# A mixture-of-experts stage that gathers raw rows and scales them afterwards, with an eighth down-weight buffer and three dummy matmuls moved

## The chip, the core and the metric

The kernel is one program on 1 NeuronCore of one Trainium2 chip. The metric is the device time of one execution in microseconds (us). Five engines run their own instruction streams and meet at semaphores: TensorE (PE), VectorE (DVE), ScalarE (ACT), GpSimd (POOL) and SyncE (SP). SP issues nearly all plain transfers; POOL issues the indirect ones. All transfers share the core's 16 DMA engines.

## The reference, cut to what matters

The reference is two transformer blocks, one after the other, on one sequence of 512 tokens of width 1024, all in float32. The change touches only the end of the second block, its mixture of experts:

```python
def rms_norm_2(x, g):
    y = x * lax.rsqrt(jnp.mean(x * x, axis=-1, keepdims=True) + EPS)
    return y * g

# in second_block, after the mixer has updated x
h = modulate(rms_norm_2(x, norm2_g[l]), shift2, scale2)      # h * (1 + scale) + shift
x = x + gate2[:, None, :] * hierarchical_moe(h, ...)
return rms_norm_2(x, final_norm_g)

def hierarchical_moe(h, ...):           # T = 512 tokens, 32 experts in 4 groups, top 2
    ...                                 # router: group, then two experts in it, weights
    order = jnp.argsort(flat_e)         # the 1024 (token, expert) pairs, by expert
    ...
    xg = ht[slot_tok].reshape(n_blocks, MOE_BLOCK, D)         # gathered token rows
    def run_block(args):
        xb, e, wb = args
        a = jax.nn.silu(xb @ w_gate[e]) * (xb @ w_up[e])      # 1024 -> 256
        return (a @ w_down[e]) * wb[:, None]                  # 256 -> 1024
    out = lax.map(run_block, (xg, blk_expert, slot_w))
    y = jnp.zeros((T, D)).at[slot_tok].add(out)
```

The root of the norm, `rsqrt(mean(x*x) + EPS)`, is one number per token. It can be multiplied into a row before it is gathered or after.

## The kernel before, in words

**The stage.** For the experts the kernel works in blocks of 64 rows (`BS`). Blocks 0 to 31 belong to experts 0 to 31. An expert with more than 64 rows gets further blocks, which run in a loop of up to 16 turns (`OVER`); in the profiled input two of them are needed. Block b goes like this:

- POOL gathers the 64 rows of block b from DRAM into the tile `raw` (line 860, `raw<-xn_rows,arena`). Four buffers (`AHEAD`) hold gathered rows: the gather for block b + 4 is issued once the rows of block b have been turned.
- PE turns the 64 rows in eight transposes (`rows_turned`, line 2806), DVE multiplies and adds the modulation (`scale_shift`, lines 2098 and 2100).
- PE multiplies with gate and up (`gate_up`, line 2790, 32 records in the profile), ACT makes a tanh of the gate half (line 1304), DVE finishes the product (lines 2105, 2107).
- PE turns that (`act_turned`, line 2813), ACT copies it to SBUF (line 1296), PE multiplies with down (`down`, line 2798). DVE applies the residual gate (line 2114) and POOL scatters the rows to `y_rows` (line 865).

PE runs ahead by one block: gate and up of block b, then the turned product, the rows of block b + 2 and the down product of block b - 1.

**The weights.** Gate and up of one expert are one transfer of 2 MB (`expert_gu`, line 626), down is one of 1 MB (`expert_dn`, line 630). There are 7 buffers for each (`NSLOT`). SP's program sets their order. In its steady loop it waits until gate and up of block b are multiplied, issues gate and up of expert b + 7, waits until down of block b is multiplied, and issues down of expert b + 7. Ahead of that loop it issues the first seven of each by hand, in between other work: the transfers of down 2 and 3, gate/up 4, the copy of the residual tile `X` to DRAM (`x_spill`, line 702), a copy of the normed rows to DRAM (`xn_rows`, line 704), down 4 and 5, gate/up 5, then a wait for the first two gathers, down 6, and gate/up 6.

**The routing.** Between the last dense matmul and the first expert block lies the routing: a chain of small DVE instructions with a few small matmuls, which ends in `slot_i` (the token of each slot) and, later, `bexp_i` (the experts of the loop's blocks). The normed rows that the gathers read are made by ACT (line 1285, four instructions) and stored by SP. In the chain's gaps PE runs matmuls that nothing reads (`hold`, line 2754): 10, then 7, then 5 ahead of the first turned rows, and 3 behind the first two blocks' rows.

**The end.** After the last block, `x_spill` comes back to `X`, the two expert rows of each token are read from `y_rows`, weighted and added, and the final norm is written out.

Of the kernel before, what the change touches and what calls it, by code (L numbers as in the profile page):

```python
# [26 lines left out]
P = 128  # L27
# [46 lines left out]
NSLOT = 7  # L74
WS = 4
# [202 lines left out]
def build(nc, x, wp, par_d, con_d, smw_d, bias_d, par2_d, smw2_d, tab2_d, tab3_d, wexp, out):  # L278
    with ExitStack() as ctx:
# [38 lines left out]
        x_spill = nc.dram_tensor("x_spill", (P, NT * D), F32).ap()  # L318
# [161 lines left out]
        def AT(n):  # L480
            at[0] += n
            assert at[0] <= 18560
            return AR(at[0] - n, n)

# [10 lines left out]
        w1c, w2c = AT(NT), AT(NT)  # L495
# [11 lines left out]
        bexp_i = AT(OVER).bitcast(I32)  # L507
        slot_i = AT(NBLK + AHEAD).bitcast(I32)
        pair_i = AT(NBLK + AHEAD).bitcast(I32)
# [4 lines left out]
        idxc, idxp = AT(WS).bitcast(I32), AT(WS).bitcast(I32)  # L514
        nblkf = AT(1)
        nblk_i = AT(1).bitcast(I32)
        actf = AT(2 * P).rearrange("p (u n) -> p u n", u=2)
# [9 lines left out]
        ssf, msf, rsf = AT(NT), AT(NT), AT(NT)  # L527
        ssf2 = AT(NT)
# [80 lines left out]

        def over_slot(v):  # L610

            s = (NE - WS + v) % NSLOT
            return s, 16 * len(range(s, NE, NSLOT))

# [8 lines left out]
        def _(sp):  # L623
# [4 lines left out]
            def expert_dn(b):  # L628

                sp.dma_start(wdn[b % NSLOT], wexp[b, :, 2 * PIECE:WE]).then_inc(S(f"down_loaded{b % NSLOT}"), 16)  # L630
# [10 lines left out]
            for n, p in enumerate(ORDER):  # L641
# [39 lines left out]
                if p == ("wout", 0):  # L681
                    sp.wait_ge(S("values_summed"), A0 + len(aunits))
                    sp.dma_start(X[:, :], x_spill).then_inc(S("x_back"), 16)
# [18 lines left out]
            sp.dma_start(x_spill, X[:, :]).then_inc(S("x_spilled"), 16)  # L702
            sp.wait_ge(S("rows_normed"), NT)
            sp.dma_start(xn_rows.rearrange("(t p) n -> p t n", p=P), xn).then_inc(S("xn_stored"), 16)
# [4 lines left out]
            for v in range(2):  # L709
                sp.wait_ge(S(f"xg_loaded{v}"), 16)  # L710
            expert_dn(6)
            sp.wait_ge(S("x_spilled"), 32)
            expert_gu(6)
            for b in range(NE - NSLOT):
# [3 lines left out]
                expert_dn(b + NSLOT)  # L718
            sp.wait_ge(S("bexp_ready"), 1)
            blocks = sp.value_load(nblk_i[0:1, :], min_val=0, max_val=OVER)  # L720
            with sp.Fori(0, OVER // WS) as i:
                for v in range(WS):
                    with sp.If(WS * i + v < blocks):
# [5 lines left out]
                        sp.wait_ge(S("y_ready"), NE - WS + WS * i + v + 1)  # L729
                        sp.dma_start(wdn[s].rearrange("p (o n) -> p o n", o=1),  # L730
                                     wexp[bass.ds(e, 1), :, 2 * PIECE:WE].rearrange("o p n -> p o n")).then_inc(S(f"down_loaded{s}"), 16)
            sp.wait_ge(S("up_ready"), 28)
            sp.dma_start(X[:, :], x_spill).then_inc(S("x_back"), 16)
# [18 lines left out]
        def _(pool):  # L752
# [118 lines left out]
            for b in range(NE + 3):  # L871
# [3 lines left out]
                if b >= 3:  # L875
                    pool.wait_ge(S("y_copied"), b - 2)
                    scatter((b - 3) % 2, pair_i[:, b - 3:b - 2])
            pool.wait_ge(S("bexp_ready"), 1)
            blocks = pool.value_load(nblk_i[0:1, :], min_val=0, max_val=OVER)
            with pool.Fori(0, OVER // WS) as i:  # L880
                for v in range(WS):
                    with pool.If(WS * i + v < blocks):
# [4 lines left out]
                        pool.wait_ge(S("idx_ready"), 2 * (WS * i + v) + 2)  # L887
# [16 lines left out]
        def _(act):  # L904
# [372 lines left out]
            for t in range(2):  # L1277
                act.activation(xn[:, t, :], Xv[:, t, :], ACT.Square, accum_out=ss2[:, t:t + 1])
            for n in range(5):
                turned(n)  # L1280
            act.activation(xn[:, 2, :], Xv[:, 2, :], ACT.Square, accum_out=ss2[:, 2:3]).then_inc(S("ss_x"), 1)
# [1747 lines left out]
```

## Time and profile before

| | us |
|---|---|
| median of 3 runs | 1617.65 |
| lowest and highest | 1617.4, 1620.41 |
| the profiled execution | 1618.26 |
| its span in the profile | 1616.4 |

The profile is of one execution. Its span, from the first to the last recorded instruction, is 1.86 us shorter than that execution's own time. Over the whole span PE is busy for 1513.8 us, DVE for 777.5, POOL for 585.6 and ACT for 455.3. The mean granted clock of PE is 0.976 of its full 2.4 GHz. The experts take the last fifth of the span, from about 1320 us.

### The profile page before, as it was taken

Reading aid. Unit: us, or ns where it says so; the run is one execution under the profiler, and the core shown is the slowest. Engines: PE = TensorE matmul, PEld = TensorE weight load, DVE = VectorE, ACT = ScalarE, POOL = GpSimd, SP = SyncE. Lnnn points to the kernel's source line nnn. Section 1 sums busy time; section 2 is a strip of 40 time slices with the busy share of each in tenths; the row PEclk is TensorE's granted clock in tenths of the full one; section 3 lists DMA queues with packets and bytes.
Section 4 is the critical chain, followed back from the end, with each engine's and each line's share of the span. In section 5 each row is a group of like instructions: output and inputs, shape, how many; then the busy total and the mean of one; then the engine's idle time right before and its main releaser. Section 6 shows DMA issues by size and latency. Waiting matters only on the chain.

```text
span 1616.4 us, 21298 instructions
## 1 busy us (share of the span) xinstructions
PE 1513.8 (94%) x8362; PEld 1197.2 (74%) x8362; DVE 777.5 (48%) x1490; ACT 455.3 (28%) x734; POOL 585.6 (36%) x483
## 2 busy tenths in 40 slices
PE   7999998999999999999999999999999989977785
PEld 6978887878888888877888888775688866544452
DVE  5565657278686863244615601445313354432234
ACT  4342335242231323252313332342223210000001
POOL 5551220435454444543633154520244313322122
PEclk9998999999999999999999999999999999999998
DMA  4340110325445442232221122310043799999995
GB/s 175 110 186 27 53 53 1 131 107 205 183 156 209 158 181 104 97 118 78 90 98 67 42 79 104 101 51 15 27 182 130 276 357 361 372 397 369 395 410 204
DMA packets 37348, 260.92 MB, mean 161 GB/s; under 512 B 7280, under 2 KB 7920, under 8 KB 13184
## 3 DMA queue, kind: packets, MB, share of 16 engines
q1 hardware_dynamic: 31488, 251.13, 41.1%
q0 software_dynamic: 5760, 8.41, 1.6%
q8 instruction: 68, 1.11, 0.3%
q14 instruction: 32, 0.26, 0.0%
HBM read 252.69 MB, written 17.30 MB: 167 GB/s over the span
## 4 chain that ended last, share of the span: by engine, by line
PE 84%; DVE 7%; issue 4%; ACT 3%; POOL 1%; DMA 1%; DVEq 0%; SPq 0%; ACTq 0%; POOLq 0%
PE G L2205 13%; PE G L2207 13%; PE G L2206 13%; PE SA L2790 4%; PE G L2790 4%; PE SA L2205 3%; PE SA L2207 3%; PE SA L2206 3%; PE PB L2207 3%; PE PB L2205 3%; PE PB L2206 3%; PE OB L2402 2%; PE G L2253 1%; PE SA L2670 1%; PE PB L2798 1%
## 5 line engine op out<-in xcount | busy, mean ns | idle before, releaser
L769 POOL TENSOR_TENSOR wl<-raw,wh 128x512 fp32r<-128x512 f32 x352 | 477.1, 1388 | 685.1 <-ACT wh L920 675.4
L920 ACT ACTIVATE wh<-raw 128x2048 fp32r<-128x2048 f32 x90 | 172.3, 1915 | 284.4 <-PE SA L2207 145.3
L2205 PE MATMUL G<-Hh,wh 128*128 128x512 f32 x544 | 217.3, 399 | 1.7 <-DVE arena L1613 1.4
L2207 PE MATMUL G<-Hh,wl 128*128 128x512 f32 x544 | 213.6, 393 | 0.0
L2206 PE MATMUL G<-Hl,wh 128*128 128x512 f32 x544 | 213.4, 392 | 0.0
L1684 DVE SCALAR_TENSOR_TENSOR arena<-arena,st 128x256 f32<-128x256 f32 x144 | 133.0, 923 | 5.1
L2205 PEld LDWEIGHTS G<-Hh,wh 128*128 128x128 f32 x544 | 103.2, 190 | 22.4 <-issue 2.2
L2207 PEld LDWEIGHTS G<-Hh,wl 128*128 128x128 f32 x544 | 103.0, 189 | 22.4
L2206 PEld LDWEIGHTS G<-Hl,wh 128*128 128x128 f32 x544 | 103.1, 190 | 19.6
L860 POOL DMA_INDIRECT raw<-xn_rows,arena x38 | 36.6, 963 | 130.9 <-PE G L2806 106.7
L2205 PE MATMUL G<-wh,Hh 128*128 128x256 f32 x256 | 77.3, 302 | 1.2 <-POOL wl L769 1.2
L2207 PE MATMUL G<-wh,Hl 128*128 128x256 f32 x256 | 72.7, 284 | 0.0
L2206 PE MATMUL G<-wl,Hh 128*128 128x256 f32 x256 | 72.6, 284 | 0.0
L2205 PE MATMUL G<-Yh,wh 128*128 128x512 f32 x168 | 65.6, 390 | 1.6 <-DVE Yl L1880 1.6
L865 POOL DMA_INDIRECT y_rows<-arena x34 | 34.5, 1014 | 87.1 <-DVE arena L2114 83.1
L1006 ACT ACTIVATE arena<-arena,st 128x128 f32<-128x128 f32 (+3 forms) x64 | 35.9, 561 | 104.8 <-DVE st L1572 104.8
L2207 PE MATMUL G<-Yh,wl 128*128 128x512 f32 x168 | 65.4, 389 | 0.0
L2206 PE MATMUL G<-Yl,wh 128*128 128x512 f32 x168 | 65.4, 389 | 0.0
L1581 DVE COPY arena<-PB 128x128 f32<-128x128 f32 (+3 forms) x64 | 31.3, 489 | 51.6 <-PE PB L2392 51.3
L2205 PE MATMUL SA<-wh,Yh 128*128 128x512 f32 x134 | 53.6, 400 | 0.0
L2207 PE MATMUL SA<-wh,Yl 128*128 128x512 f32 x134 | 52.4, 391 | 0.0
L2205 PEld LDWEIGHTS G<-wh,Hh 128*128 128x128 f32 x256 | 49.2, 192 | 4.2 <-issue 2.9
(536 smaller groups left out, 3094.6 us busy)
## 6 DMA issues: line engine op xcount, KB each, us to landing
raw<-in_pieces_dram SPq DMA_DIRECT2D x91, 1024.0 KB, 4.8
arena<-in_pieces_dram SPq DMA_DIRECT2D x24, 1024.0 KB, 4.8
arena<-in_wexp_dram SPq DMA_DIRECT2D x11, 2048.0 KB
dn_w<-in_wexp_dram SPq DMA_DIRECT2D x18, 1024.0 KB, 41.4
arena<-in_wexp_dram SPq DMA_DIRECT2D x12, 1024.0 KB
gu_y<-in_wexp_dram SPq DMA_DIRECT2D x6, 2048.0 KB
gu_z<-in_wexp_dram SPq DMA_DIRECT2D x5, 2048.0 KB
gu_h<-in_wexp_dram SPq DMA_DIRECT2D x4, 2048.0 KB, 37.8
```

Source lines behind the costliest of these rows:

```text
L769: ins = pool.tensor_tensor(low_[:, part], whole[:, part], high[:, part], ALU.subtract)
L860: pool.indirect_dma_start(xg(v), None, xn_rows, bass.IndirectOffsetOnAxis(ap=index, axis=0), bounds_check=T - 1, oob_is_err=False).then_in ...
L865: pool.indirect_dma_start(y_rows, bass.IndirectOffsetOnAxis(ap=index, axis=0), yb[:, u, :], None, bounds_check=4 * T - 1, oob_is_err=False ...
L920: act.activation(split_pair(s)[0], wait_raw(act, sp_list[s]), ACT.Copy).then_inc(S("high_split"), 1)
L1006: act.activation(SP[:, u % 2, 0:nk], SP[:, u % 2, 0:nk], ACT.Exp, scale=-1.0, bias=nmax[:, u % 2:u % 2 + 1], accum_out=rsum[:, ((u // 8) % ...
L1581: dve.tensor_copy(PTs[:, u % 2, 0:nk], PB[u % 2][:, 0:nk]).then_inc(S("pt_copied"), 1)
L1684: own(dve.scalar_tensor_tensor(a, w[:, k, :], condc[:, k:k + 1], a, ALU.mult, ALU.add))
L2205: pe.matmul(out, ah, bh, start=first, stop=False)
L2206: pe.matmul(out, ah, bl, start=False, stop=False)
L2207: return pe.matmul(out, al, bh, start=False, stop=last)
L2402: ins = pe.matmul(OB[:, h * HD:(h + 1) * HD], PTs[:, u % 2, k * P:(k + 1) * P], Zv[:, k, ty, (h // 4) * HD:(h // 4 + 1) * HD], start=k == ...
L2790: ins = pe.matmul(GU[u][BS * j:BS * j + BS, 0:256], xgT[:, u, k, :], wg[:, j, k, :], start=k == 0, stop=k == KT - 1)
```

## The change

Four things change.

1. The normed copy of the rows is gone: ACT's four instructions, their DRAM tensor and SP's transfer. The gathers read `x_spill`, the raw rows, which is now laid out by token. The root is multiplied into each gathered block by ACT, in place in `raw` (`rows_scaled`), and PE waits for that (`xg_scaled`) in place of the gather. ACT does it for block b + 2, ahead of the tanh of block b.
2. The root of each slot (`row_rstd`) is found like its token: DVE makes `slot_rstd` in two instructions, PE multiplies it with `place` in 16 small matmuls, DVE copies the result. POOL copies the column for each block of the loop.
3. An eighth buffer for down weights (`NDOWN`) lies in the routing's temporaries; the small tables that live on have moved to the end of the arena (`KEPT`). The first seven are issued in another order: down 6 goes ahead of gate/up 4, gate/up 6 no longer comes behind a wait for two gathers, and down 7 follows once the routing is done. The steady loop then issues gate/up of expert b + 7 and down of expert b + 8.
4. The three dummy matmuls behind the first rows are put ahead of them: `hold(8)` in place of `hold(5)` and `hold(3)`.

```diff
+NDOWN = 8
...
-        xn_rows = nc.dram_tensor("xn_rows", (T, D), F32).ap()
         y_rows = nc.dram_tensor("y_rows", (2 * T * 2, D // 2), F32).ap()
-        xn = raw[:, :].rearrange("p (t n) -> p t n", t=NT)
+        sq_act, sq_vec = raw[:, 0:D], raw[:, D:2 * D].unsqueeze(1).to_broadcast([P, NT, D])
+        slot_one = AR(13824, 8 * (NBLK + 2)).rearrange("p (c n) -> p c n", c=8)
+        slot_rstd = AR(14336, 8 * (NBLK + 2)).rearrange("p (c n) -> p c n", c=8)
...
+        row_rstd = KEPT(NBLK + AHEAD)
+        over_rstd = KEPT(WS)
...
+        wdn.append(AR(low_at[0] - PIECE, PIECE))
+        assert low_at[0] - PIECE >= 14848 + 1024
...
             wait_used(sp, ("wout", 2))
             expert_dn(2)
             expert_dn(3)
+            sp.wait_ge(S("low_split"), len(split_pieces()))
+            expert_dn(6)
             wait_group(sp, "wout", 7)
             expert_gu(4)
             wait_freed(sp, "wout", 7)
-            sp.dma_start(x_spill, X[:, :]).then_inc(S("x_spilled"), 16)
-            sp.wait_ge(S("rows_normed"), NT)
-            sp.dma_start(xn_rows.rearrange("(t p) n -> p t n", p=P), xn).then_inc(S("xn_stored"), 16)
+            sp.dma_start(x_spill_tiles, Xv).then_inc(S("x_spilled"), 16)
             expert_dn(4)
             expert_dn(5)
             wait_group(sp, "gr", 0)
             expert_gu(5)
-            for v in range(2):
-                sp.wait_ge(S(f"xg_loaded{v}"), 16)
-            expert_dn(6)
             sp.wait_ge(S("x_spilled"), 32)
             expert_gu(6)
+            sp.wait_ge(S("bexp_ready"), 1)
+            expert_dn(7)
             for b in range(NE - NSLOT):
                 sp.wait_ge(S("up_ready"), b + 1)
                 expert_gu(b + NSLOT)
                 sp.wait_ge(S("y_ready"), b + 1)
-                expert_dn(b + NSLOT)
-            sp.wait_ge(S("bexp_ready"), 1)
+                if b + NDOWN < NE:
+                    expert_dn(b + NDOWN)
...
-            pool.wait_ge(S("xn_stored"), 16)
+            pool.wait_ge(S("x_spilled"), 32)
...
-                pool.indirect_dma_start(xg(v), None, xn_rows, bass.IndirectOffsetOnAxis(ap=index, axis=0),
+                pool.indirect_dma_start(xg(v), None, x_spill, bass.IndirectOffsetOnAxis(ap=index, axis=0),
...
+                        pool.tensor_copy(over_rstd[:, v:v + 1], row_rstd[:, bass.ds(b + AHEAD, 1)]).then_inc(S("idx_ready"), 1)
...
-            act.wait_ge(S("rstd_x"), 6)
-            for t in range(NT):
-                act.activation(xn[:, t, :], Xv[:, t, :], ACT.Copy, scale=rstd2[:, t:t + 1]).then_inc(S("rows_normed"), 1)
...
+            def rows_scaled(b, v, scale):
+
+                act.activation(xg(v), xg(v), ACT.Copy, scale=scale).then_inc(S("xg_scaled"), 1)
+
+            act.wait_ge(S("places_ready"), 3)
+            for b in range(2):
+                act.wait_ge(S(f"xg_loaded{b}"), 16)
+                rows_scaled(b, b, row_rstd[half_rows(b), b:b + 1])
             for b in range(NE):
+                v = (b + 2) % AHEAD
+                act.wait_ge(S(f"xg_loaded{v}"), xg_count(b + 2))
+                rows_scaled(b + 2, v, row_rstd[half_rows(v), b + 2:b + 3])
                 if b >= 1:
                     turned_copy(b - 1)
                 act.wait_ge(S("up_ready"), b + 1)
...
                         act.wait_ge(S("tanh_free"), b - 1)
                         act.activation(tanhg[:, u, :], GU[u][0:BS, 0:256], ACT.Tanh, scale=0.5).then_inc(S("tanh_ready"), 1)
+                        n = (v + 2) % WS
+                        act.wait_ge(S(f"xg_loaded{n}"), xg_count(NE) + 16 * i + 16 * ((v + 2) // WS))
+                        rows_scaled(b + 2, n, over_rstd[half_rows(n), n:n + 1])
                         act.wait_ge(S("act_turned"), b + 1)
...
+            for k in range(2):
+                ins = dve.tensor_tensor(slot_rstd[:, 4 * k:4 * k + 4, :], slot_one[:, 4 * k:4 * k + 4, :],
+                                        rstd2.unsqueeze(2).to_broadcast([P, NT, NBLK + 2]), ALU.mult)
+            ins.then_inc(S("places_ready"), 1)
...
+            dve.wait_ge(S("slots_rooted"), 1)
+            own(dve.tensor_copy(row_rstd[:, 0:NBLK + 2], SA[1][:, 0:NBLK + 2]))
+            dve.tensor_copy(over_rstd, row_rstd[:, NE:NE + WS]).then_inc(S("places_ready"), 1)
...
+            pe.wait_ge(S("places_ready"), 2)
+            for c in range(8):
+                for u in range(2):
+                    ins = pe.matmul(SA[1][BS * u:BS * u + BS, 0:NBLK + 2], place[:, c, :], slot_rstd[:, c, :], start=c == 0, stop=c == 7)
+            ins.then_inc(S("slots_rooted"), 1)
...
-                pe.wait_ge(S(f"xg_loaded{b % AHEAD}"), xg_count(b))
+                pe.wait_ge(S("xg_scaled"), b + 1)
...
-            hold(5)
+            hold(8)
             rows_of(0)
             rows_of(1)
-            hold(3)
```

How the order moves, on three engines. On SP, the transfers between the last weights of the dense part and the steady loop, before (`gu` tiles and 128x4096 are gate/up weights, 128x2048 are down weights, `X` is the seventh gate/up buffer):

```order
L630 DMA dn_w<-in_wexp_dram 128x2048 x2
L626 DMA gu_h<-in_wexp_dram 128x4096
L702 DMA x_spill<-X 128x4096
L704 DMA xn_rows<-raw 128x4x1024
L630 DMA dn_w<-in_wexp_dram 128x2048 x2
L626 DMA gu_l<-in_wexp_dram 128x4096
L630 DMA raw<-in_wexp_dram 128x2048
L626 DMA X<-in_wexp_dram 128x4096
L626 DMA arena<-in_wexp_dram 128x4096
L630 DMA arena<-in_wexp_dram 128x2048
```

And the same place now:

```order
L652 DMA dn_w<-in_wexp_dram 128x2048 x2
L652 DMA raw<-in_wexp_dram 128x2048
L648 DMA gu_h<-in_wexp_dram 128x4096
L726 DMA x_spill<-X 128x4x1024
L652 DMA dn_w<-in_wexp_dram 128x2048 x2
L648 DMA gu_l<-in_wexp_dram 128x4096
L648 DMA X<-in_wexp_dram 128x4096
L652 DMA arena<-in_wexp_dram 128x2048
L648 DMA arena<-in_wexp_dram 128x4096
L652 DMA arena<-in_wexp_dram 128x2048
```

The 2 MB of `xn_rows` are gone, down 6 (`raw`) moved up by five transfers, and a new 1 MB transfer (down 7, `arena`) stands ahead of the first of the steady loop.

On PE, from the matmuls that look up the slots to the first expert block, before (`SA<-con` are the dummy matmuls, `G<-con,raw` the turned rows, `G<-arena 64x256` gate and up of block 0):

```order
L2778 MATMUL G<-arena 64x50 x16
L2781 MATMUL OB<-arena,con 128x16
L2754 MATMUL SA<-con 128x256 x5
L2806 MATMUL G<-con,raw 128x64 x16
L2754 MATMUL SA<-con 128x256 x3
L2790 MATMUL G<-arena 64x256 x16
```

And now:

```order
L2820 MATMUL G<-arena 64x50 x16
L2825 MATMUL SA<-arena 64x50 x16
L2828 MATMUL OB<-arena,con 128x16
L2796 MATMUL SA<-con 128x256 x8
L2853 MATMUL G<-con,raw 128x64 x16
L2837 MATMUL G<-arena 64x256 x16
```

Sixteen small matmuls are new (line 2825), and nothing stands any more between the turned rows and gate and up of block 0.

On ACT, from the routing's last exponential into the expert blocks, now (`raw<-raw,arena` scales a block of gathered rows, 64x256 is the tanh, 128x128 the copy of the turned product):

```order
L1310 ACTIVATE arena<-arena 128x4
L1321 ACTIVATE raw<-raw,arena 64x1024 x3
L1336 ACTIVATE arena<-G 64x256
L1321 ACTIVATE raw<-raw,arena 64x1024
L1317 ACTIVATE arena<-SA 128x128
L1336 ACTIVATE arena<-SA 64x256
```

Before, these places held only the tanh and the copies. Each scaling stands in the queue ahead of the copy of the block before and of the tanh of the same turn.

## Rows read from the trace of the kernel before

**Rows 1.** The page, share of 16 DMA engines in 40 slices, in tenths.
```profile
DMA  4340110325445442232221122310043799999995
```

**Rows 2.** Windows: stretch, length, busy us of each engine, PE clock, DMA share, GB/s.
```profile
1316.00:1324.00 8.00, 6.17 (x34) 4.78 (x34) 4.09 (x12) 0.00 (x0) 5.76 (x6) 0.87 0.58 194
1284.00:1336.00 52.00, 45.06 (x314) 33.49 (x315) 27.92 (x84) 11.98 (x21) 8.99 (x10) 0.93 0.90 342
...
1400.00:1563.00 163.00, 126.52 (x914) 75.25 (x912) 53.33 (x95) 12.32 (x38) 35.52 (x36) 0.93 1.01 387
```

**Rows 3.** Waits of PE, 1315 to 1592 us: total, times, longest.
```profile
PE SA L2790 <- issue: 16.5, 6, 4.2
PE G L2790 <- issue: 13.4, 7, 3.4
```

**Rows 4.** Timeline of SP's transfers: start, us in issue, line, out<-in, count.
```profile
1282.20 0.80 SPq L630 DMA_DIRECT2D dn_w<-in_wexp_dram  x2
1290.37 0.33 SPq L626 DMA_DIRECT2D gu_h<-in_wexp_dram  x1
...
1300.10 0.39 SPq L704 DMA_DIRECT2D xn_rows<-raw  x1
...
1320.75 0.33 SPq L630 DMA_DIRECT2D raw<-in_wexp_dram  x1
...
1328.49 0.33 SPq L626 DMA_DIRECT2D arena<-in_wexp_dram  x1
1335.38 0.33 SPq L630 DMA_DIRECT2D arena<-in_wexp_dram  x1
```

**Rows 5.** The page's DMA queues: packets, MB, share of 16 engines.
```profile
q0 software_dynamic: 5760, 8.41, 1.6%
```

**Rows 6.** DMA issues, 1281 to 1284 us: KB each, us to landing.
```profile
dn_w<-in_wexp_dram SPq DMA_DIRECT2D x2, 1024.0 KB, 4.8
```

**Rows 7.** The chain of waits around the first expert block: start, us, what.
```profile
1316.47 4.00 DMA raw<-xn_rows,arena
...
1320.51 1.21 PE G L2806 x16
1321.71 2.67 PE SA L2754 x6
1324.38 4.06 PE G L2790 x32
...
1329.09 3.60 PE SA L2790 x32
```

**Rows 8.** PE's timeline before the first turned rows: start, us, line, count.
```profile
1313.81 1.14 PE L2778 MATMUL G<-arena 128*64 128x50 f32 x32 [1.02 <-DVE arena L2070]
1316.26 2.42 PE L2754 MATMUL SA<-con 128*128 128x256 f32 x10
```

**Rows 9.** DVE's timeline at the routing's end.
```profile
1315.37 0.26 DVE L2075 TENSOR_SCALAR arena<-G,arena 128x50 int32<-128x50 f32 x1
...
1317.41 0.24 DVE L2090 CAST arena<-arena 128x16 int32<-128x16 f32 x1
```

**Rows 10.** ACT's timeline: the normed copies, and the tanh of block 32.
```profile
1295.81 4.27 ACT L1285 ACTIVATE raw<-X,st 128x1024 f32<-128x1024 f32 x4 [0.93 <-POOL st L777]
...
1575.66 0.38 ACT L1314 ACTIVATE arena<-G 64x256 f32<-64x256 f32 x1 [5.61 <-PE G L2790]
```

**Rows 11.** PE's timeline in the first of the loop's two blocks.
```profile
1575.48 0.43 PE L2841 MATMUL G<-con,raw 64*128 64x64 f32 x2
1575.75 0.60 PE L2806 MATMUL G<-con,raw 64*128 64x64 f32 x7
1577.00 0.43 PE L2841 MATMUL SA<-con,arena 64*128 64x64 f32 x2 [0.65 <-DVE arena L2107]
```

**Rows 12.** POOL's timeline at the end: the last scatters.
```profile
1581.54 1.01 POOL L865 DMA_INDIRECT y_rows<-arena  x1 [3.69 <-DVE arena L2137]
1587.83 0.18 POOL L885 COPY arena<-arena 64x1 int32 x1 [5.28 <-DMA y_rows<-arena]
```

More of the change, by code:

```diff
@@ L317, in build @@
         smw2 = arena[:, 0:SMW2["_"][1]]
-        x_spill = nc.dram_tensor("x_spill", (P, NT * D), F32).ap()
+        x_spill = nc.dram_tensor("x_spill", (T, D), F32).ap()
+        x_spill_tiles = x_spill.rearrange("(t p) n -> p t n", p=P)
         Xv = X[:, :].rearrange("p (t n) -> p t n", t=NT)
@@ L481, in AT, with KEPT @@
             at[0] += n
-            assert at[0] <= 18560
+            assert at[0] <= low_at[0]
             return AR(at[0] - n, n)
+        low_at = [18560]
+        def KEPT(n):
+            low_at[0] -= n
+            return AR(low_at[0], n)
         def v3(n):
@@ L494, in build @@
         assert at[0] >= 14848 + 1024
-        w1c, w2c = AT(NT), AT(NT)
+        w1c, w2c = KEPT(NT), KEPT(NT)
         cntc, nbc, pend = AT(1), AT(1), AT(1)
@@ L506, in build @@
         block_tok = AR(12288 + 8 * BS, 8 * (NBLK + 2)).rearrange("p (c n) -> p c n", c=8)
-        bexp_i = AT(OVER).bitcast(I32)
-        slot_i = AT(NBLK + AHEAD).bitcast(I32)
-        pair_i = AT(NBLK + AHEAD).bitcast(I32)
+        bexp_i = KEPT(OVER).bitcast(I32)
+        slot_i = KEPT(NBLK + AHEAD).bitcast(I32)
+        pair_i = KEPT(NBLK + AHEAD).bitcast(I32)
         slot_f = AT(NBLK + AHEAD)
+        row_rstd = KEPT(NBLK + AHEAD)
+        over_rstd = KEPT(WS)
         second = AT(8)
@@ L513, in build @@
         dst_i = AT(8).bitcast(I32)
-        idxc, idxp = AT(WS).bitcast(I32), AT(WS).bitcast(I32)
+        idxc, idxp = KEPT(WS).bitcast(I32), KEPT(WS).bitcast(I32)
         nblkf = AT(1)
-        nblk_i = AT(1).bitcast(I32)
-        actf = AT(2 * P).rearrange("p (u n) -> p u n", u=2)
+        nblk_i = KEPT(1).bitcast(I32)
+        actf = KEPT(2 * P).rearrange("p (u n) -> p u n", u=2)
         tanhg, acth = (AR(14848 + n, 512)[BS:P].rearrange("p (u n) -> p u n", u=2) for n in (0, 512))
@@ L608, in slot_count, with down_count, over_down @@
             return 16 * (b // NSLOT) + 16
+        def down_count(b):
+            return 16 * (b // NDOWN) + 16
+        def over_down(v):
+            s = (NE - WS + v) % NDOWN
+            return s, 16 * len(range(s, NE, NDOWN))
         def over_slot(v):
@@ L877, in _ @@
                     scatter((b - 3) % 2, pair_i[:, b - 3:b - 2])
+            pool.wait_ge(S("places_ready"), 3)
             pool.wait_ge(S("bexp_ready"), 1)
@@ L1277, in _ @@
             for t in range(2):
-                act.activation(xn[:, t, :], Xv[:, t, :], ACT.Square, accum_out=ss2[:, t:t + 1])
+                own(act.activation(sq_act, Xv[:, t, :], ACT.Square, accum_out=ss2[:, t:t + 1]))
             for n in range(5):
                 turned(n)
-            act.activation(xn[:, 2, :], Xv[:, 2, :], ACT.Square, accum_out=ss2[:, 2:3]).then_inc(S("ss_x"), 1)
+            act.activation(sq_act, Xv[:, 2, :], ACT.Square, accum_out=ss2[:, 2:3]).then_inc(S("ss_x"), 1)
             turned(6)
-            act.wait_ge(S("rstd_x"), 6)
-            for t in range(NT):
-                act.activation(xn[:, t, :], Xv[:, t, :], ACT.Copy, scale=rstd2[:, t:t + 1]).then_inc(S("rows_normed"), 1)
             act.wait_ge(S("group_shifted"), 1)
@@ L2067, in _ @@
             iota_b = cols(tab3, TAB3, "iota_b").unsqueeze(1).to_broadcast([P, 8, NBLK + 2])
-            own(dve.tensor_tensor(block_tok, iota_b, dst_b.unsqueeze(2).to_broadcast([P, 8, NBLK + 2]), ALU.is_equal))
-            own(dve.tensor_tensor(block_tok, block_tok, second.unsqueeze(2).to_broadcast([P, 8, NBLK + 2]), ALU.mult))
+            own(dve.tensor_tensor(slot_one, iota_b, dst_b.unsqueeze(2).to_broadcast([P, 8, NBLK + 2]), ALU.is_equal))
+            own(dve.tensor_tensor(block_tok, slot_one, second.unsqueeze(2).to_broadcast([P, 8, NBLK + 2]), ALU.mult))
             dve.tensor_tensor(place, cols(tab3, TAB3, "iota_r").unsqueeze(1).to_broadcast([P, 8, BS]),
                               dst_r.unsqueeze(2).to_broadcast([P, 8, BS]), ALU.is_equal).then_inc(S("places_ready"), 1)
+            for k in range(2):
+                ins = dve.tensor_tensor(slot_rstd[:, 4 * k:4 * k + 4, :], slot_one[:, 4 * k:4 * k + 4, :],
+                                        rstd2.unsqueeze(2).to_broadcast([P, NT, NBLK + 2]), ALU.mult)
+            ins.then_inc(S("places_ready"), 1)
             b = wait_group(dve, "slots", 0)
@@ L2829, in turn_and_down @@
                     pe.wait_ge(S("y_copied"), b - 1)
-                down(b, b % 2, b % NSLOT)
+                down(b, b % 2, b % NDOWN)
             def rows_of(b):
-                pe.wait_ge(S(f"xg_loaded{b % AHEAD}"), xg_count(b))
+                pe.wait_ge(S("xg_scaled"), b + 1)
                 if b >= 2:
@@ L2873, in _ @@
                         act_turned(u, turned_by_matmul)
+                        s, before = over_down(v)
                         pe.wait_ge(S(f"down_loaded{s}"), before + 16 * i + 16)
```

21 lines of the change are left out of this document (11 added, 10 removed).

## The prediction

> **What bounds the kernel now.** I read the page's row of DMA shares first. From slice 32 on, some 1290 us, it stands at 7 to 9 tenths [rows 1]. The windows say how full that is: between 1400 and 1563 us the 16 engines are busy all the time (share 1.01) at 387 GB/s, while PE is busy for 126.52 of 163 us [rows 2]. The waits agree: PE's largest before gate and up go to "issue", 16.5 and 13.4 us [rows 3], and what ends them is a landed weight, which the profile does not name as a releaser. So in the expert stage the end is set by the transfers. It is late by whatever time the DMA engines stood empty before and by every byte that need not have moved. PE's start counts only through the issues that hang on it.
>
> Two places are left where the engines were not full: between 1316 and 1324 us, share 0.58 [rows 2], while SP held back down 6 and gate/up 6 for the first gathers, and just before gate/up 4 is issued at 1290.37 [rows 4]. The window 1284 to 1336 us moved 52 x 342 = 17.8 MB [rows 2].
>
> **How far before's queue reaches at 1336 us.** SP's issues from 1282.20 to 1328.49 us are eleven pieces of work, 17 MB of 1.049 million bytes, 17.8 MB; six of the issues are shown [rows 4]. Next to them run eight gathers. All 72 gathers and scatters together moved 8.41 MB [rows 5], 0.12 MB each, so about 0.9 MB. Of 18.7 MB, 17.8 were moved: 0.8 MB, or 2.1 us at 387 GB/s, were still queued at 1336 us, when down 7 (issued at 1335.38) joined.
>
> **The same queue after the change.** Removed are 2.1 MB of `xn_rows`, 5.4 us at 387 GB/s. Down 6 fills the gap before 1290.37 us. Gate/up 6 takes the place of the copy, so the queue is empty at about the same time as before, some 1318 us. Down 7 follows at the routing's end and is through by about 1325. But then SP has nothing that it may issue: gate/up 7 needs block 0's gate and up, down 8 needs block 0's down. The gain is cut to what those two waits allow, so I work out when block 0 runs.
>
> - The slot lookup gets 16 more small matmuls. They stand behind `slot_i`'s, which took 1.14 us from 1313.81 [rows 8], so they end at 1316.1. The first gather does not wait for them. DVE's two products of 128x200 fall into its gap while PE multiplies. Its copies of the roots come behind the instruction that ends at 1315.63 [rows 9]: it waits 0.5 us and copies for 0.4 us. The routing ends 0.95 us later, at 1318.6 instead of 1317.65 [rows 9]. What hides this is the first gather, in flight from 1316.47 for 4.00 us [rows 7]; without that cover it costs 0.95 us.
> - The dummy matmuls took 2.42 us for five [rows 8], 0.48 each. Eight, from 1317.2, end at 1321.1.
> - The first gather lands at 1320.5, and ACT then scales it. No 64x1024 instruction is in the trace. Four of 128x1024 took 4.27 us, 1.07 each, the upper bound, and the tanh of 64x256 took 0.38, the lower [rows 10]. As time goes by the elements in a row, I take 1.07. The rows are ready at 1321.6, after the dummy matmuls: these hide.
> - Turning one block is half of 1.21 us [rows 7], then DVE needs 1.4 us (the gap from 1321.1 to 1322.5 in the same step before). Gate and up of block 0 start at about 1323.8 instead of 1324.38: the scaling costs 1.07, and three dummy matmuls of 2.67 us no longer stand behind the rows [rows 7].
> - PE's pause before the rows was 1.82 us (from 1318.69 to 1320.51), and a lower level followed: the granted clock of 1316 to 1324 us is 0.87 [rows 2], and three dummy matmuls took 2.67 us there instead of 1.45. Now the pauses are about 0.5 us each. I take block 0's gate and up at the 3.60 us of block 1, not 4.06 [rows 7]. They end at 1327.4, and block 0's down at 1334.2: 1.1 us earlier than the issues at 1328.49 and 1335.38 [rows 4].
>
> A transfer of 1 MB lands 4.8 us after its issue into an empty queue [rows 6]. Moving takes 2.6 of that, so down 8 starts to move some 2.1 us after its issue, at 1336.3 us. Gate/up 7, issued at 1327.4, is just through by then. From here both kernels move the same up to gate/up 31: 24 down and 24 gate/up transfers, since the eighth buffer puts down 31 ahead of gate/up 31. That is why the buffer itself brings nothing there: its megabyte comes off the lead. The lead is 2.1 us less 0.3: **1.8 us** as a mean over the engines, the lower bound. The upper bound is the whole price of the copy, 5.4 us. The truth is above the mean, since a weight has landed only when the slowest of 16 engines has its part, and the emptied queue lets all 16 start level, while gathers and weights no longer cross between 1321 and 1330 us. I take **4.0 us**, nearer the upper end.
>
> **What comes back at the end.** In the two blocks of the loop PE turns the rows of block b + 2 right behind gate and up. Now ACT first does its tanh (until 1576.04), then scales for 1.07 us [rows 10]. PE turns at 1577.15 and needs 0.87 us (from 1575.48 to 1576.35), until 1578.0. The turned product, which ran at 1577.00 [rows 11], waits for that: 1.0 us. The same again in the second block: **2.0 us**. For blocks 0 to 31 the scaling costs nothing: it lies under gate and up of the next block (3.60 us), and a gather has three to four blocks of time. POOL's third copy per turn of the loop lies under its wait for the scatter, 5.28 us [rows 12]. The raw rows in DRAM go in pieces of 4 KB both ways; I put that at nothing, with 0.3 us per 2 MB as bound, covered by the queue's slack in the dense part.
>
> Sum: -4.0 + 2.0 = -2.0 us. Against the profiled execution, 1618.26 us (span 1616.4), that is 1616.3. It stood 0.6 above the median of the runs; on the median, 1617.65, it is **1615.7 us**.
>
> **A rule that speaks against this.** The issue of the first gather now meets a queue that may still hold gate/up 6. Two indirect transfers show the spread: 4.00 us from issue to use for the first gather, in a nearly empty queue [rows 7], and 6.3 us for the scatter issued at 1581.54, whose landing POOL met at 1587.83 [rows 12]. The Trainium skill (DMA: Bandwidth & Descriptors, Queues, rings and completion order) says that each engine goes round-robin between the queue rows that have work, a packet at a time. By that rule a gather waits for a packet and not for the 2 MB, and the first gather stays near 4 us; if it had to wait for the whole queue, block 0 would start up to 5 us later. The 6.3 us lie between the two and settle neither.
>
> **The rivals.**
> - *The lead is larger* (28 in 100). The slowest engine keeps the whole 5.4 us, block 0's 1.1 us earlier issues come on top, and of the loop's 2.0 us one is hidden, because the last scatter had waited for POOL: its predecessor landed at 1587.83 only [rows 12], in a queue that is now empty sooner. -5.4 - 1.1 + 1.0 = -5.5: 1612.2 us. For it: the share of 1.01 leaves no room for a lead to be lost. Against it: PE's chain, not POOL, sets the final sum.
> - *The first gather is late* (14 in 100). Before, SP held 3 MB back until two gathers had landed; now 2 MB may be ahead and down 7 beside it. If the gather lands 5 us later, PE pauses for 5 us more and does block 0 at its lower clock, 1.5 us longer. Every us moves the issues of gate/up 7 and down 8, with the queue empty: -2.0 + 6.5 = +4.5, 1622.2 us. It decides from 2 us of delay (no gain) and is measurable from 5.2. Against it: the queue's end at 1318 us lies ahead of 1320.5.
> - *The lead is lost before the end* (8 in 100): only the mean of 1.8 us holds and the loop takes its 2.0: +0.2, 1617.9 us.
> - That the change does not do what it says I exclude: the copy's instructions are out of the order.
>
> **How the numbers follow.** A measurement of this kernel tells a difference from none above about 0.2%, 3.2 us. The forecast has 50 in 100, with its own range 1613.8 to 1617.5; 7 of these lie below 1614.4. Faster by over 0.2%: 7 and 26 of the first rival, 33. Slower: 12 of the second rival. The rest, 55, is within 0.2%. The range reaches from the larger lead to a gather 4 us late: 1612.0 to 1619.5.
>
> **What would show it.** Right: four fewer ACT instructions and one fewer SP transfer; the DMA share high up to about 1318 us, a hole between about 1325 and 1330 us, then no hole until 1560; gate/up 7 issued near 1327.4; gate and up of block 31 some 4 us earlier than at 1563; each block of the loop 1.0 us longer, with PE waiting for ACT's scaling before the turned rows. Wrong: a first gather of over 5 us, gate and up of block 0 after 1324.4, a PE that waits for ACT's scaling within blocks 3 to 31, or a hole in the DMA share after 1340.

## The result, and the profile after

| | before | after |
|---|---|---|
| median of 5 runs each, us | 1618.36 | 1626.29 |
| lowest and highest, us | 1617.4, 1621.43 | 1623.04, 1626.69 |
| profiled execution, its span, us | 1618.26, 1616.4 | 1623.04, 1621.2 |

The ratio is 1.0042 (95% interval 1.003 to 1.0053): the changed kernel is slower by 0.3 to 0.5%, beyond what a measurement can tell from none. The forecast was 1615.7 us in a range of 1612.0 to 1619.5. A second comparison of the same kernel gave 1.0029 (1.0017 to 1.0041). The profiled execution is the fastest of the five after, so its trace shows less of the loss than the medians do.

The page's row of DMA shares, where [rows 1] had it:

```profile
DMA  4350110325445442232222022310043879999994
```

As forecast the queue is full from slice 34 on. The windows of the changed kernel, with the columns of [rows 2], show the hole that was forecast and its real size:

```profile
1284.00:1336.00 52.00, 42.85 (x304) 32.90 (x304) 26.50 (x84) 11.65 (x19) 7.35 (x9) 0.90 0.79 298
1320.00:1324.00 4.00, 2.68 (x18) 1.96 (x16) 0.00 (x0) 1.15 (x1) 2.24 (x3) 1.00 0.84 299
1324.00:1328.00 4.00, 0.95 (x8) 0.93 (x8) 1.42 (x2) 2.12 (x2) 0.94 (x1) 0.82 0.37 86
1328.00:1332.00 4.00, 4.00 (x22) 2.19 (x21) 1.42 (x2) 0.17 (x1) 0.93 (x1) 0.50 0.05 11
1332.00:1336.00 4.00, 4.00 (x34) 2.53 (x32) 1.11 (x3) 1.41 (x2) 0.23 (x1) 0.83 0.33 66
1336.00:1340.00 4.00, 4.00 (x40) 2.53 (x36) 1.49 (x3) 1.04 (x3) 0.71 (x1) 1.00 0.90 377
1400.00:1563.00 163.00, 130.21 (x960) 77.66 (x958) 54.70 (x98) 35.21 (x60) 37.37 (x38) 0.94 1.01 389
```

Over the 12 us from 1324 to 1336 the share is 0.37, 0.05 and 0.33, a quarter on average. The forecast had the hole from about 1325 to 1330; it lasts until 1336. PE's granted clock is 0.50, the lower level of 1.2 GHz, in the middle of it. SP's timeline has the issues around it, here those of gate/up 4, gate/up 6, down 7, gate/up 7 and down 8 (start, us in issue, line, transfer); [rows 4] has those of before:

```profile
1291.71 0.33 SPq L648 DMA_DIRECT2D gu_h<-in_wexp_dram  x1
...
1306.63 0.33 SPq L648 DMA_DIRECT2D X<-in_wexp_dram  x1
1319.64 0.33 SPq L652 DMA_DIRECT2D arena<-in_wexp_dram  x1
1334.41 0.33 SPq L648 DMA_DIRECT2D arena<-in_wexp_dram  x1
1341.30 0.33 SPq L652 DMA_DIRECT2D arena<-in_wexp_dram  x1
```

Gate/up 7 is issued 42.70 us after gate/up 4 (1334.41 less 1291.71). The forecast had 37.0 (1327.4 less the 1290.37 of [rows 4]), and down 8 at 43.8; it came at 49.6. Both are late by 5.7 us. The chain of waits says why (start, us, what; pieces of up to 0.04 us are left out), beside [rows 7]:

```profile
1319.41 6.42 DMA raw<-x_spill,arena
...
1325.85 1.16 ACT raw L1321
...
1327.05 1.12 PE G L2853 x8
1328.17 6.19 PE G L2837 x32
1334.36 0.64 PE G L2853 x8
1335.00 3.60 PE SA L2837 x32
```

The chain goes back to the *second* gather, block 1's, not to the first. ACT's timeline and PE's show both (op, out<-in, and in brackets the idle time before and its releaser):

```profile
1322.05 1.15 ACT L1321 ACTIVATE raw<-raw,arena 64x1024 f32<-64x1024 f32 x1 [16.68 <-DMA raw<-x_spill,arena]
1325.85 2.32 ACT L1321 ACTIVATE raw<-raw,arena 64x1024 f32<-64x1024 f32 x2 [2.65 <-DMA raw<-x_spill,arena]
```

```profile
1323.25 0.71 PE L2853 MATMUL G<-con,raw 64*128 64x64 f32 x8 [1.28 <-ACT raw L1321]
1327.05 1.12 PE L2853 MATMUL G<-con,raw 64*128 64x64 f32 x8 [3.09 <-ACT raw L1321]
```

The first gather is issued at 1317.89 and scaled at 1322.05, 4.16 us later. The second was issued at 1319.41, 0.23 us ahead of down 7, and ACT could use it only 6.42 us later. PE turns block 1's rows before it multiplies block 0's, so it stood for 3.09 us. Block 0's gate and up then took 6.19 us at the lower clock, where before had 4.06 [rows 7] and the forecast 3.60.

### The profile page after: what moved, and what is told of

It is laid out like the page before. It is cut to its first block, busy times and chain, and to the rows that moved or that the text cites. A ratio compares the mean times of both kernels' runs of the same rounds, so it can differ in the third digit from the quotient of the medians.

```text
span 1621.2 us, 21407 instructions
## 1 busy us (share of the span) xinstructions
PE 1516.4 (94%) x8394; PEld 1198.8 (74%) x8394; DVE 779.7 (48%) x1494; ACT 491.0 (30%) x766; POOL 584.6 (36%) x485
## 3 DMA queue, kind: packets, MB, share of 16 engines
q0 software_dynamic: 5760, 8.41, 1.6%
q8 instruction: 68, 1.11, 0.3%
## 4 chain that ended last, share of the span: by engine, by line
PE 84%; DVE 6%; issue 4%; ACT 3%; POOL 1%; DMA 1%; DVEq 0%; SPq 0%; ACTq 0%; POOLq 0%
PE G L2247 13%; PE G L2249 13%; PE G L2248 13%; PE G L2837 4%; PE SA L2837 4%; PE SA L2247 3%; PE SA L2249 3%; PE SA L2248 3%; PE PB L2249 3%; PE PB L2248 3%; PE PB L2247 3%; PE OB L2444 2%; PE G L2295 1%; PE SA L2712 1%; PE OB L2845 1%
## 5 line engine op out<-in xcount | busy, mean ns | idle before, releaser
L882 POOL DMA_INDIRECT raw<-x_spill,arena x38 | 36.5, 961 | 129.8 <-PE G L2853 106.4
L1087 ACT ACTIVATE arena<-G 128x512 f32<-128x512 f32 x32 | 19.2, 599 | 115.4 <-PE G L2249 115.4
```

The lines of the kernel that those rows point to most:

```text
L882: pool.indirect_dma_start(xg(v), None, x_spill, bass.IndirectOffsetOnAxis(ap=index, axis=0), bounds_check=T - 1, oob_is_err=False).then_in ...
```

## The experiments

To compare profiles I count from the issue of gate/up 4. Its absolute time is set in the dense part, whose matmuls no kernel here changes, and it moves between profiles: 1290.37 before, 1291.71 after, 1288.93 to 1295.06 in the others. That this is hardly the change's doing shows far ahead of the experts. A chain piece of the dense part that is the same in all kernels starts at 294.70 us in after, at 293.30 in before and, in a kernel whose dense part is before's line for line (`b1` below), at 292.57:

```profile
294.70 3.46 PE G L2489 x32
```

```profile
293.30 3.46 PE G L2447 x32
```

```profile
292.57 3.47 PE G L2447 x32
```

From the profile of each kernel, in us after the issue of gate/up 4: block 0's gate and up, the issue of gate/up 8, the start of block 31's gate and up; then the time from there to the end of the span.

| | block 0 starts, takes | gate/up 8 issued | block 31 starts | to the end | median, before in the same series | ratio (95%) |
|---|---|---|---|---|---|---|
| before | 34.01, 4.06 | 45.38 | 272.82 | 53.2 | | |
| after | 36.46, 6.19 | 49.96 | 273.03 | 56.5 | 1626.29, 1618.36 | 1.0042 (1.003 to 1.0053) |
| a1 | 36.15, 5.35 | 48.81 | 273.20 | 58.0 | 1624.92, 1619.98 | 1.0029 (1.0017 to 1.0041) |
| a2 | 34.32, 5.36 | 46.99 | 270.75 | 58.2 | 1620.94, 1619.98 | 1.0004 (0.999 to 1.0018) |
| a3 | 32.95, 3.67 | 44.12 | 272.05 | 58.2 | 1625.69, 1619.98 | 1.0027 (1.0016 to 1.0038) |
| a4 | 36.78, 5.95 | 50.03 | 274.29 | 54.8 | 1620.56, 1619.98 | 1.0006 (0.9996 to 1.0017) |
| a8 | 33.94, 5.36 | 46.61 | 269.95 | 52.9 | 1616.87, 1619.62 | 0.9985 (0.9974 to 0.9996) |
| a7 | 34.31, 5.36 | 48.60 | 272.87 | 53.3 | 1619.34, 1619.62 | 1.0003 (0.9992 to 1.0013) |
| a9 | 34.13, 5.36 | 46.80 | 270.73 | 55.2 | 1618.13, 1619.62 | 0.9985 (0.9971 to 1.0) |
| b1 | 32.82, 3.67 | 43.80 | 272.13 | 54.8 | 1619.4, 1619.62 | 0.9997 (0.9985 to 1.0009) |
| c1 | 34.17, 3.67 | 45.15 | 269.49 | 53.3 | 1616.85, 1619.86 | 0.9978 (0.9969 to 0.9988) |
| c2 | 36.08, 6.35 | 49.74 | 273.41 | 56.4 | 1624.12, 1619.86 | 1.003 (1.0019 to 1.0041) |

The medians are of 11 or 12 executions (after: 5), and each profile is of one. The two can lie far apart: a2's executions took 1616.18 to 1626.24 us, and the profiled one, 1624.95, is 4.0 above their median; c1's is 2.8 above its median, a8's 2.1 below.

**a1: the changed kernel again,** with no edit, for a shared base.

> The changed kernel once more, as the base of the others. Every theory: 1623 to 1627 us, 5 to 8 us above the kernel before. Theory A (the second gather meets down 7 and holds up block 0) expects the second gather to be waited for about 6 us from its issue, against some 2 us in the kernel before, and gate and up of block 0 some 10 us after the first gather's issue. Theory B (the loss lies in the loop's two blocks at the end, where PE waits for ACT's scaling) expects about 1 us for each of the two and the rest of the difference there too.

The slowdown is there again. As theory A said, the second gather is used 6.12 us after its issue and block 0's product starts 10.0 us after the first gather's. In this profile both of the last down products ran slowly, 3.61 and 3.64 us where before has 1.94 and 1.95:

```profile
1579.70 3.61 PE PB L2845 x8
...
1589.91 3.64 PE OB L2845 x8
```

The windows of the first of them, in a1 and in before (columns as above), show the clock: 0.50 against 1.00.

```profile
1579.70:1583.10 3.40, 3.40 (x8) 1.08 (x10) 0.72 (x2) 0.00 (x0) 0.00 (x0) 0.50 0.29 118
```

```profile
1577.90:1579.80 1.90, 1.89 (x10) 0.88 (x12) 0.49 (x1) 0.00 (x0) 0.00 (x0) 1.00 0.52 209
```

**a2: down 7 waits for the first two gathers.**

```diff
             sp.wait_ge(S("bexp_ready"), 1)
+            for v in range(2):
+                sp.wait_ge(S(f"xg_loaded{v}"), 16)
             expert_dn(7)
```

> Down 7 is issued only when the first two gathers have landed; gate/up 6 stays as it is. Theory A (down 7, issued 0.2 us behind the second gather, is what delays it): the second gather lands some 3 us earlier, gate and up of block 0 start 3 us earlier and at the full clock more often, gate/up 7 is issued 4 to 6 us earlier; since the queue stands empty there, the whole gains 3 to 5 us. Theory A2 (gate/up 6 is what delays the gathers): no change here, within 1 us. Theory B (the loop at the end): no change.

1620.94 us, 4.0 less than a1. ACT now scales three blocks without a gap, so the second gather is no longer late:

```profile
1325.06 3.36 ACT L1323 ACTIVATE raw<-raw,arena 64x1024 f32<-64x1024 f32 x3 [17.20 <-DMA raw<-x_spill,arena]
```

One transfer of 1 MB, issued 0.23 us behind a gather, cost that. The time fell by what theory A said (3 to 5 us), but its steps were smaller than it said: block 0 starts 1.8 us earlier than in a1 and not 3, still takes 5.36 us at the lower clock, and gate/up 8 goes out 1.8 us earlier; block 31 starts 2.5 us earlier. So the profiles show 2.5 of the 4.0 us. The 4.0 are uncertain themselves: from the 12 times of each kernel, the 95% interval of the gain is 0.7 to 6.3 us.

**a3: the same wait one transfer earlier,** ahead of gate/up 6 (before's own arrangement).

```diff
             sp.wait_ge(S("x_spilled"), 32)
+            for v in range(2):
+                sp.wait_ge(S(f"xg_loaded{v}"), 16)
             expert_gu(6)
```

> Gate/up 6 and down 7 are both issued only when the first two gathers have landed, as down 6 and gate/up 6 were in the kernel before. Theory A: block 0 no earlier than with down 7 alone behind the wait (within 0.5 us), and the queue stands empty for some 5 us before the gathers but is full from 1322 us on, so within 1.5 us of that run. Theory A2 (gate/up 6 delays the gathers): only here block 0 comes earlier, by 3 us, and the time falls by 3 to 5 us. Theory B: no change in either.

1625.69 us, no gain, where A had it within 1.5 us of a2 and A2 3 to 5 us under a1: both missed. Block 0 has the best start of all (32.95, at the full clock), and yet block 31 is 1.3 us later than in a2. The window, columns as above, shows why:

```profile
1316.00:1324.00 8.00, 6.22 (x83) 5.30 (x84) 3.74 (x18) 1.30 (x2) 3.73 (x4) 1.00 0.11 31
```

The engines moved 31 GB/s for 8 us, while 3 MB of weights were held back. From gate/up 4 on, the profiles of a3 and a2 end 1.3 us apart, the medians 4.7 (interval 0.8 to 6.8); what the rest is I did not show. The run also shows what a queue that is not empty costs the first gather: from issue to use it takes 3.34 us here, with nothing ahead of it, and 4.16 to 4.69 in the nine kernels with gate/up 6 ahead. But it took 4.04 in before and 4.45 in b1 too, where SP held gate/up 6 back and the tail of earlier transfers was still moving: the DMA share of before from 1316.25 to 1317.25 us is 1.11. So the 0.7 to 1.4 us are those of any tail and not the change's. The second gather took 6.04 to 6.76 us in the four kernels that issue down 7 behind it (after, a1, a4, c2), and at most 3.9 in a8 (issued at 1317.74; ACT takes it up at about 1321.6, right behind the first): down 7 costs it at least 2 us.

**a4: in the loop, ACT scales ahead of its tanh.** Its wait for the gather and `rows_scaled` stand above the wait for gate and up instead of behind the tanh.

```diff
                     with act.If(WS * i + v < blocks):
-                        act.wait_ge(S("up_ready"), b + 1)
-                        act.wait_ge(S("tanh_free"), b - 1)
-                        act.activation(tanhg[:, u, :], ...)
                         n = (v + 2) % WS
                         ...
                         rows_scaled(b + 2, n, over_rstd[half_rows(n), n:n + 1])
+                        act.wait_ge(S("up_ready"), b + 1)
+                        act.wait_ge(S("tanh_free"), b - 1)
+                        act.activation(tanhg[:, u, :], ...)
```

> In the loop's blocks ACT scales the rows of block b + 2 ahead of its wait for gate and up of block b, so under PE's matmuls, and not behind the tanh. Nothing else changes. Theory B: PE no longer waits 1.6 us twice; each of the two blocks is 0.85 us shorter, and since the end follows PE here, the whole gains 1.7 us, up to 3 if a pause less keeps PE's clock up. Theory A alone: no change, within 0.5 us.

1620.56 us, 4.4 less than a1 (interval 2.6 to 5.5), where theory B had 1.7, up to 3. The prediction had put the scaling at 2.0 for both blocks. In after's chain it stands twice, and a slow down product behind it:

```profile
1573.65 3.47 PE G L2837 x32
...
1577.62 1.15 ACT raw L1321
1578.82 0.43 PE G L2888 x2
...
1582.32 3.47 PE SA L2837 x32
...
1586.17 1.14 ACT raw L1321
1587.36 0.43 PE G L2888 x2
...
1588.93 3.28 PE OB L2845 x8
```

Block 32's gate and up to block 33's: 8.67 us, against 7.76 in before (from 1572.09 to 1579.85). That is 0.9 for this block, against the forecast's 1.0. With the edit PE's pause for ACT (1.71 us) is gone and the turned product waits only 0.66 us, as in before; the very last down product is slow all the same in this profile (granted clock 0.62).

```profile
1577.03 0.43 PE L2888 MATMUL SA<-con,arena 64*128 64x64 f32 x2 [0.66 <-DVE arena L2149]
...
1585.69 3.01 PE L2845 MATMUL OB<-dn_w,arena 128*64 128x512 f32 x8 [0.41 <-issue]
```

**a8: a2 and a4 together.**

> Both single repairs together: down 7 behind the landing of the first two gathers, and ACT's scaling in the loop ahead of its wait. If the two costs are separate places, their gains of 4.0 and 4.4 us add up: about 8 us under the changed kernel, 2 to 4 us under the kernel before. If both only bought the same thing (a pause less for PE's clock), together they gain no more than 5 us and the kernel is level with the one before.

1616.87 us. Against before in its own series that is -2.8 us, a1 had +4.9: 7.7 us for both repairs, where 4.0 and 4.4 add up to 8.3. Within the noise they add, and what remains is faster than before by 0.15%, near the forecast's 2.0 us. Block 0's gate and up still ran mostly at the lower clock (0.50 from 1325 to 1328 us):

```profile
1321.71 0.71 PE L2855 MATMUL G<-con,raw 64*128 64x64 f32 x8 [1.42 <-ACT raw L1323]
...
1323.97 5.36 PE L2839 MATMUL G<-arena 128*64 128x256 f32 x32 [0.51 <-DVE arena L2144]
```

**a7: a8, and block 1's rows turned behind block 0's gate and up.**

```diff
             rows_of(0)
-            rows_of(1)
             for b in range(NE):
...
                 if b == 0:
+                    rows_of(1)
                     rows_of(2)
```

> As the one with both repairs, and PE turns the rows of block 1 behind gate and up of block 0, not ahead of them. If block 0 is held up only by the second gather and its scaling, which stand ahead of it in PE's order, gate and up of block 0 start when the first block is scaled, turned and modulated, some 2 to 3 us earlier than in that run, gate/up 7 is issued as much earlier, and the whole gains 1 to 2.5 us more (to some 1614 to 1615 us). Rival: gate and up of block 1 then wait for block 1's rows, so that down 8 is issued no earlier, and nothing is gained.

1619.34 us: it gives a8's gain back, and the rival was right. Block 0 gained nothing (34.31 against 33.94): from its first turned row to its product are 2.25 us in a7 and 2.26 in a8, which is the turning of its own rows and DVE's work on them. So once the second gather is on time, block 1's rows ahead of block 0's product cost nothing. Block 1's gate and up must now wait for DVE's work on its rows, and gate/up 8 goes out at 48.60 instead of 46.61:

```profile
1325.27 5.36 PE G L2839 x32
...
1331.32 0.70 DVE arena L2142
...
1332.82 3.67 PE SA L2839 x32
```

**a9: a4 with seven down buffers,** the order of the steady loop as in before.

```diff
-NDOWN = 8
+NDOWN = 7
...
             expert_gu(6)
-            sp.wait_ge(S("bexp_ready"), 1)
-            expert_dn(7)
             for b in range(NE - NSLOT):
...
                     expert_dn(b + NDOWN)
+            sp.wait_ge(S("bexp_ready"), 1)
```

> Only seven down buffers: down 7 is issued in the steady loop, behind down of block 0, as before the change; ACT's scaling in the loop stands ahead of its wait. The forecast's account (the eighth buffer puts down 31 ahead of gate/up 31 and brings nothing by itself) expects the same time as the run with both repairs, within 1 us: the second gather meets no down 7 here either. A theory in which the eighth transfer fills the empty stretch of the queue and is worth its 2.7 us expects this one 2 to 3 us slower than that run.

1618.13 us against 1619.62, ratio 0.9985 (0.9971 to 1.0), the same ratio as a8 with its eight buffers; the medians differ by 1.3 us, the starts of block 31 by 0.8. That agrees with the forecast, by which the eighth buffer brings nothing. It doesn't settle it: the interval of a9 less a8 is -1.5 to 3.0 us, so a gain of 2 us is not excluded. Put in without a wait, the buffer costs what a2 took away.

**b1: the kernel before with the dummy matmuls moved alone.**

```diff
-            hold(5)
+            hold(8)
             rows_of(0)
             rows_of(1)
-            hold(3)
```

> The kernel before, with nothing changed but the dummy matmuls: eight ahead of the first turned rows and none behind. The forecast's account expects gate and up of block 0 to start some 0.5 us later than they could but at the full clock (3.6 us, not 4.06), gate/up 7 issued 0 to 1 us earlier, and the whole within 1 us of the kernel before. If the three moved matmuls cost by delaying the rows (they end at 1320.1 with the first gather at 1320.5, so nearly never), up to 1 us slower.

1619.4 against 1619.62: no change, although block 0 starts 1.2 us earlier and at 3.67 us. Block 31 starts only 0.7 earlier: in before's queue, which is not empty there, an earlier issue is passed on only in part.

**c1: a8 with twelve dummy matmuls** instead of eight.

```diff
-            hold(8)
+            hold(12)
             rows_of(0)
```

> Both repairs, and twelve dummy matmuls ahead of the first turned rows instead of eight, 1.9 us more at 0.48 each, so that they end at about the moment at which the second block is scaled. Theory: PE's pause there is what put block 0's gate and up at the lower clock (5.36 us against 3.67). It should take 3.7 us, up to 0.5 us later in its start, gate/up 7 and 8 are issued 1.2 to 1.7 us earlier, and since the queue is empty there, gate and up of block 31 and the end come as much earlier than in the run with both repairs: some 1615.5 us, 4 us under the kernel before. Rival: the queue is no longer empty there, and nothing moves behind block 0.

1616.85 against 1619.86: 0.9978 (0.9969 to 0.9988), the lowest ratio of all and faster than both kernels, by 3.0 us where 4 were expected. The pause ahead of the first turned rows is gone, and block 0 runs at the full clock:

```profile
1321.60 5.45 PE L2798 MATMUL SA<-con 128*128 128x256 f32 x24
...
1327.89 0.71 PE L2855 MATMUL G<-con,raw 64*128 64x64 f32 x8 [0.21 <-ACT raw L1323]
1329.23 3.67 PE L2839 MATMUL G<-arena 128*64 128x256 f32 x32 [0.63 <-DVE arena L2144]
```

Gate/up 8 goes out 1.5 us earlier than in a8, but block 31 starts only 0.5 earlier, and the interval overlaps a8's: what the clock at block 0 is worth for the whole is not resolved.

**c2: the changed kernel with twelve dummy matmuls alone.** The same edit, on after.

> The changed kernel with twelve dummy matmuls instead of eight and nothing else. If the whole loss at block 0 were the clock, this alone would bring 1.7 us or more. Theory A expects that the second gather, late by down 7, still holds up block 0's start (some 36 us after gate/up 4's issue), with the dummy matmuls ending 3 us before it, so that PE pauses all the same and gate and up take more than 5 us: gain under 1 us.

1624.12 against 1619.86, 1.003: no gain. The second gather is still late, PE pauses for 2.33 us ahead of block 1's rows, and its granted clock, 1.00 until then, is 0.53 from 1326 to 1327.4 us and 0.50 after that:

```profile
1317.85 5.45 PE L2796 MATMUL SA<-con 128*128 128x256 f32 x24
...
1326.27 1.11 PE L2853 MATMUL G<-con,raw 64*128 64x64 f32 x8 [2.33 <-ACT raw L1321]
```

## Why the prediction was wrong

**The failed step: the start of block 0.** "Gate and up of block 0 start at about 1323.8" and "I take block 0's gate and up at the 3.60 us of block 1" were both wrong. I followed the first gather only. Block 0's product stands in PE's order behind the rows of block 1 as well, so it waits for the second gather and its scaling, and that gather met down 7, which the forecast's sum had put at nothing. From gate/up 4 on, the start came at 36.46 instead of 33.4, and the length was 6.19 instead of 3.60: 5.6 us in all. Of these a8 takes back 2.5 us of the start, and c1 the length. With the second gather on time, block 1's rows cost block 0 nothing (a7): the term that was missing is the late gather, not the order alone.

The rest of the start, 0.5 to 0.9 us in a8 and a2, is mostly the first gather, in use 4.30 and 4.69 us after its issue instead of 4.0. The forecast called the queue in which it had measured the 4.00 "nearly empty"; the trace shows a share of 1.11 in the first us behind that issue. What an empty queue gives is a3's 3.34.

**The lead was near its size, by extrapolation.** Where the queue runs empty, block 31 starts an almost fixed time after gate/up 8 is issued: 223.1 to 224.4 us in nine kernels (after, a1, a2, a4, a7, a8, a9, c1, c2), 223.9 on average. So, within those 1.3 us, each us that block 0 is late is a us at the end. With gate/up 8 at the forecast 44.2, block 31 would start at 268.1, 4.7 us earlier than in before; the forecast said 4.0, a value that it had chosen between 1.8 and 5.4 and not worked out, so that its closeness is partly luck. No run has that case; the nearest is c1, with gate/up 8 at 45.15 and a lead of 3.3. With gate/up 8 at 49.96 nothing of it is left: 273.03 against 272.82.

**The ending cost 3.3 us, not 2.0.** The scaling took 1.15 us (1.07 was forecast). Along the chain, the first of the loop's blocks took 0.9 us more than in before and the second 0.8, which is the forecast's 2.0. Not forecast was the clock: the last down product took 3.28 us instead of 1.95 at a granted clock of 0.57, +1.3. DVE's turns of the loop that are skipped took 5.05 us where before has 4.41, +0.6, and what comes behind them took 0.4 less.

```profile
1598.08 0.87 DVE L2182 TENSOR_SCALAR arena<-con,arena 128x128 f32<-128x128 f32 x4 [5.05 <-issue]
```

```profile
1592.84 0.87 DVE L2140 TENSOR_SCALAR arena<-con,arena 128x128 f32<-128x128 f32 x4 [4.41 <-issue]
```

The ten kernels built on the changed program all have the 5.05 us, before and b1 the 4.41. What follows is 0.5 us shorter in the ten, on average, so that little of it reaches the end.

A slow down product is not the change's alone. With ACT's scaling behind the tanh (after, a1, a2, a3, c2), 8 of the loop's 10 down products took 2.83 to 3.64 us; in the seven other kernels of the table 3 of 14 did, 3.01 to 3.11 (a4, a9, b1). From block 31 to the end the five took 56.4 to 58.2 us, 57.5 on average, the seven 52.9 to 55.2, 53.9 on average. The difference, 3.5 us, agrees with what a4 gave back (4.4 by its median). The scalings are 1.7 of it and the clock the likeliest part of the rest; why the clock falls in one profile and not in another stays open.

The sum by profile: 1.34 (dense part, hardly the change) + 0.21 (up to block 31) + 3.25 (the end) = +4.8 us. The medians say +7.9 and, in a1's comparison, +4.9. After's profiled execution is 3.25 us under its own median; where its slower executions lose more I did not show.

**The rivals.** The late gather (14 in 100) came closest. It had the mechanism (down 7 beside the gather, a pause, the lower clock, an empty queue that passes each us on), and its price, +4.5 us, is near the +4.9 of a1's comparison. But it named the first gather, which took 4.16 us in after and 4.45 in b1; the real one was the second. The larger lead needed block 0 earlier than in before, and block 0 came later. "The lead is lost" names what happened by block 31, but not its reason.

**The rule on the queues.** The Trainium skill (DMA: Bandwidth & Descriptors, Queues, rings and completion order) has the engines take packets in turn from the queue rows that have work. Gate/up 6 does not test this: in after the DMA share is 0.81 in the first us behind the issue of the first gather (1317.89 to 1318.89) and 0.38 in the next, so little was left ahead of it, and a gather that waited for all of it would have come about 1 us late as well (4.16 to 4.69 us, against 3.34 in the empty queue). Down 7 does: it was issued behind the second gather and still cost it at least 2 us, which agrees with turns and not with the order of issue. From "a gather waits for a packet and not for the 2 MB" the forecast took "near 4 us", and that does not follow for a gather of 80 packets (5760 for 72 transfers, [rows 5]), each of which, by that rule, takes its turn. How the 2 us come about in detail no run here shows.

## What to carry to other kernels

Before a wait is moved or dropped, list everything that stands in the engine's order ahead of the step you price, and follow each to its own transfer: here the second gather decided, not the first. A transfer that nothing needs soon, such as a prefetch into a new buffer, is best issued once a small gather on which the next step hangs has landed (a2, -4.0 us), but holding back all that could fill the queue gives the gain back (a3, 0). Price an added wait on TensorE with the clock of the matmuls behind it: block 0's product took 1.7 us more where PE had paused for 1.4 us ahead of the rows (a8) than where it had not (c1).

## What the runs showed of the hardware

- A gather of 64 rows of 4 KB took 3.34 us from issue to use with idle DMA engines (a3), 4.04 to 4.69 behind the tail of large transfers (the eleven other kernels), and 6.04 to 6.76 with a 1 MB transfer issued 0.23 us behind it (after, a1, a4, c2).
- TensorE's clock: after pauses of 1.42 us ahead of the first turned rows and 0.33 and 0.51 us behind them, 32 records of gate and up took 5.36 us (a8); after pauses of 0.21 and 0.63 us (c1), or of 0.94 and 1.05 (b1), 3.67 us. The loop's two down products took 1.94 and 1.95 us each in before, a7, a8 and c1; in the other kernels at least one took 2.83 to 3.64, at granted clocks of 0.50 to 0.66. Pauses of 0.65 us alone don't tell these apart (a4 and a8 have the same), so what decides there is open.
- DVE's skipped turns of the loop took 0.64 us more in the changed kernel and its nine variants (5.05) than in before and b1 (4.41). The cause is open.
